# Gate values added element by element into a zeroed DRAM matrix, instead of one-hot products; last u tiles and v products in one program block

## The reference

```python
q = (xc @ w_q).reshape(ch, PEER_HEADS, 2, half)                 # 8 heads
s = jnp.einsum('thpd,hpnd->thpn', q, sub_keys)                  # 2 x 128 scores
v1, i1 = lax.top_k(s[:, :, 0], PEER_TOPK)                       # 16 of 128
v2, i2 = lax.top_k(s[:, :, 1], PEER_TOPK)
cand = (v1[..., :, None] + v2[..., None, :]).reshape(ch, PEER_HEADS, 256)
vals, ci = lax.top_k(cand, PEER_TOPK)
e = take(i1, ci // 16) * N_KEYS + take(i2, ci % 16)             # expert, 0..16383
g = jax.nn.softmax(vals, axis=-1)
act = jax.nn.gelu(jnp.einsum('td,thkd->thk', xc, u_tab[e])) * g
return jnp.einsum('thk,thkd->td', act, v_tab[e])
```

## Time and profile before

| What | us |
|---|---|
| median of 3 runs (3643.9 to 3649.4) | 3646.4 |
| the profiled execution's own time | 3651.8 |
| its span, first to last instruction | 3650.0 |
| PE busy | 3425.3 |
| DVE busy | 2373.7 |
| ACT busy | 1380.7 |
| POOL busy | 602.3 |
| layer 0, routing: first query product to its last u tile | 277.7 to 730.4 |
| layer 0, softmax and spread blocks | 734.3 to 1180.5 |
| layer 0, v products | 1201.5 to 1749.9 |
| layer 1, routing starts; last gelu of u | 2171.8 to 3072.0 |
| layer 1, projections (from the third on) start; attention starts | 1778; 1930.3 |
| layer 1, v products | 3092.4 to 3638.9 |

### The profile page before, as it was taken

The page is one execution under the profiler, slowest core; times in us unless marked ns, Lnnn a source line. Parts: engine busy times, 40 slices in busy tenths (PEclk is TensorE's granted clock), DMA queues, the critical chain, the costliest instruction groups (busy, mean ns, idle before and its releaser), DMA issues. The chain is left out here.

```text
span 3650.0 us, 51301 instructions
## 1 busy us (share of the span) xinstructions
PE 3425.3 (94%) x16516; PEld 2789.0 (76%) x16516; DVE 2373.7 (65%) x5172; ACT 1380.7 (38%) x2002; POOL 602.3 (17%) x545
## 2 busy tenths in 40 slices
PE   8779999989999799999899879999999997999998
PEld 6557888878888677778666568888788886778776
DVE  4545676755654688888536636767645554788887
ACT  3433333234444333333425623333234443333332
POOL 0000000000000755553000000000000002755551
PEclk9889999999999899999999989999999998999999
DMA  4113343334543999999311013434335444999997
GB/s 149 50 46 120 122 147 128 125 121 159 194 169 136 324 333 331 332 332 317 119 31 47 2 48 118 141 125 144 120 117 195 168 167 171 348 335 333 336 330 246
DMA packets 303862, 663.93 MB, mean 182 GB/s; under 512 B 34320, under 2 KB 159248, under 8 KB 302224
## 3 DMA queue, kind: packets, MB, share of 16 engines
q1 hardware_dynamic: 257264, 486.34, 38.6%
q0 software_dynamic: 45056, 134.38, 11.5%
q10 hardware_dynamic: 1440, 41.94, 2.8%
HBM read 551.40 MB, written 111.15 MB: 182 GB/s over the span
## 5 line engine op out<-in xcount | busy, mean ns | idle before, releaser
L398 PE MATMUL up_ps<-up_hhi,up_hi 128*128 128x512 f32 x2048 | 809.4, 395 | 7.9 <-PEq L1726 7.9
L398 PE MATMUL up_ps<-up_hlo,up_hi 128*128 128x512 f32 x2048 | 798.4, 390 | 0.0
L398 PE MATMUL up_ps<-up_hhi,up_lo 128*128 128x512 f32 x2048 | 798.2, 390 | 0.0
L1705 POOL DMA_INDIRECT ex_gz<-gelu,ga_atz x256 | 321.2, 1255 | 2572.6 <-POOLq L2106 2495.3
L389 DVE TENSOR_TENSOR up_lo<-up_raw,up_hi 128x1024 fp32r<-128x1024 f32 x256 | 313.5, 1225 | 585.5 <-ACT up_hi L385 574.5
L2268 PE MATMUL ex_psy<-ex_vh,ex_ah 128*128 128x512 f32 x1536 | 608.0, 396 | 67.4 <-DVE ex_al L2336 66.0
L2268 PE MATMUL ex_psy<-ex_vl,ex_ah 128*128 128x512 f32 x1536 | 599.7, 390 | 0.0
L2268 PE MATMUL ex_psy<-ex_vh,ex_al 128*128 128x512 f32 x1536 | 599.2, 390 | 0.0
L406 ACT ACTIVATE up_z<-up_ps 128x512 f32<-128x512 f32 x256 | 153.1, 598 | 897.4 <-PE up_ps L398 889.5
L398 PEld LDWEIGHTS up_ps<-up_hhi,up_hi 128*128 128x128 f32 x2048 | 385.9, 188 | 84.3 <-DVE up_lo L389 8.7
L398 PEld LDWEIGHTS up_ps<-up_hhi,up_lo 128*128 128x128 f32 x2048 | 385.0, 188 | 80.7
(11 more groups left out here) (355 smaller groups left out, 4162.6 us busy)
## 6 DMA issues: line engine op xcount, KB each, us to landing
up_raw<-in_uT SPq DMA_DIRECT2D x256, 512.0 KB, 3.3
ex_vr<-in_v SPq DMA_DIRECT2D x256, 512.0 KB, 5.6
gelu<-up_z SPq DMA_DIRECT2D x256, 256.0 KB, 2.0
ex_z<-gelu SPq DMA_DIRECT2D x256, 192.0 KB, 5.6
ex_gm<-gate_matrix SPq DMA_DIRECT2D x128, 320.0 KB, 6.7
gate_matrix<-sg_gbuf ACTq DMA_DIRECT2D x6, 4096.0 KB, 12.4
ro_wq<-in_peer_wq SPq DMA_DIRECT2D x32, 512.0 KB, 4.6
gate_matrix<-ga_last ACTq DMA_DIRECT2D x4, 4096.0 KB, 12.3
```

Source lines behind the costliest of these rows:

```text
L398: last = pe.matmul(self.ps[:, a, :], w[:, a, dc, :], h[:, dc, :], start=(dc == 0 and m == 0), stop=(dc == DC - 1 and m == 2))
L1705: pool.indirect_dma_start(z[:, j:j + 1], None, zmat.rearrange("p k (t a) -> (p k t) a", a=1), bass.IndirectOffsetOnAxis(ap=self.at_z[:, j: ...
```

## The change

1. **Zeroing.** In `front0` and `front1` POOL clears the small tile `ga_at`, and ACT issues eight writes (NZERO) of it, repeated, over the whole `gate_matrix`, one after each of the projections 2 to 9. The matrix now holds all 384 tokens in one layout (128 x 128 x 384), and SP waits for the writes at the end of the front block.
2. **Routing.** DVE computes the softmax and the addresses head by head (`shift`, `place`, `give`), with the exponential on ACT. POOL writes the gates of a head with 48 indirect DMAs (3 token tiles x 16), each of 128 single elements that are added to what DRAM holds (`scatter`). Before each head but the first, POOL waits until all additions of the heads before have landed. Six heads (ROUTED) are written within the routing block.
3. **Experts.** The blocks `gate_softmax` and `spread_gates` are gone. Their 64 u tiles stand at the head of the `experts` block, followed by the v products with no block end between. POOL writes the last two heads, gathers 8 v rows, waits for the gelus, then gathers as before. SP waits for all scatters before the first load of gates. The addition of a gathered row comes one iteration (four v tiles) later than before, and the six PSUM banks are added as each ends (`ended`).

```diff
+HW = TD * TOPK
+ROUTED = 6
+NZERO = 8
...
+    def zero_gates(self, act, gmat, n, signal):
+        z = self.zeros()
+        w = NK * SD // NZERO
+        rows = gmat.rearrange("p k t -> p (k t)")[:, n * w:(n + 1) * w].rearrange("p (r c) -> p r c", c=2 * HK)
+        act.dma_start(rows, bc(z.unsqueeze(1), [P, w // (2 * HK), 2 * HK])).then_inc(signal.sem, 16)
+
+    def scatter(self, pool, gmat, to, gates, h):
+        if h > 0:
+            pool.wait_ge(self.scattered.sem, self.scattered.base + 16 * HW * h)
+        for j in range(h * HW, (h + 1) * HW):
+            pool.indirect_dma_start(gmat.rearrange("p k (t a) -> (p k t) a", a=1),
+                                    bass.IndirectOffsetOnAxis(ap=to[:, j:j + 1], axis=0), gates[:, j:j + 1], None,
+                                    compute_op=ALU.add).then_inc(self.scattered.sem, 16)
...
 def route(...)
+            for h in range(ROUTED):
+                pool.wait_ge(given.sem, given.done(h))
+                ga.scatter(pool, gmat, to, gates, h)
...
+            def exps(h):
+                act.wait_ge(shifted.sem, h + shifted.done(0))
+                act.activation(share[:], share[:], ACT.Exp).then_inc(expd.sem, 1)
...
             def give(h):
-                at = bass.ds(h * TOPK, TOPK)
-                dve.tensor_copy(key1[:, :, at], keys[:, 0, :, :])
-                dve.tensor_copy(key2[:, :, at], keys[:, 1, :, :])
-                dve.tensor_copy(valsb[:, :, at], best[:]).then_inc(selected.sem, 1)
+                here = bass.ds(h * TOPK, TOPK)
+                place()
+                dve.scalar_tensor_tensor(out=spot[:, 0:TD, :], in0=at[:, 0:TD, :], scalar=float(SD), ...)
+                dve.tensor_scalar(spot[:, TD, :], at[:, TD, :], float(S), token[:, TD:TT], ALU.mult, ALU.add)
+                dve.tensor_copy(to[:, bass.ds(h * HW, HW)], spot[:, 0:TD, :].rearrange("p t k -> p (t k)"))
...
+                dve.wait_ge(expd.sem, h + expd.done(0))
+                dve.tensor_reduce(total[:], share[:], AX.X, ALU.add)
+                dve.reciprocal(total[:], total[:])
...
 def experts(...)
         def _(sp):
...
+            for a in range(GT):
+                load_v(a, a)
+            for t in range(2 * GT):
+                load_z(t, t // GT, t % GT)
+            sp.wait_ge(ga.scattered.sem, ga.scattered.base + 16 * PH * HW)
+            for par in range(2):
+                load_g(par, par)
...
         def _(pe):
+            with pe.Fori(0, (NK - G0) // GT) as i:
+                for a in range(GT):
+                    up.product(pe, i * GT + (G0 + a), a)
...
         def _(pool):
+            for h in range(ROUTED, PH):
+                ga.scatter(pool, gmat, to, gates, h)
+            for j in range(NV):
+                ga.gather_v(pool, gv, j)
+            for s in up.kept:
+                pool.wait_ge(s.sem, s.base + s.credit + 16 * NK // GT)
             for j in range(Z_AHEAD):
                 ga.gather_z(pool, gz, zmat, j)
+            for j in range(Z_AHEAD, HK):
+                ga.gather_z(pool, gz, zmat, j)
+                ga.gather_v(pool, gv, j)
...
         def _(dve):
-                        dve.tensor_tensor(blocks[:, 0:NTB - 1, :], blocks[:, 0:NTB - 1, :], gm[:, par, :, a, :], ALU.mult)
-                        dve.tensor_tensor(blocks[:, NTB - 1:NTB, :], blocks[:, NTB - 1:NTB, :], ga.last[...], ALU.mult)...
+                        dve.tensor_tensor(zz[:, par, a, :], zz[:, par, a, :], gm[:, par, a, :], ALU.mult).then_inc(s_["mul"].sem, 1)
```

More of the change, by code:

```diff
@@ L1743, in route @@
         keys = k.sb(c, f"ro_keys{l}", [P, 2, TT, TOPK])
+        share = k.sb(c, f"ro_share{l}", [P, TT, TOPK])
+        total = k.sb(c, f"ro_total{l}", [P, TT])
+        at = k.sb(c, f"ro_at{l}", [P, TT, TOPK])
+        spot = k.sb(c, f"ro_spot{l}", [P, TT, TOPK])
+        token = k.sb(c, f"ro_token{l}", [P, TT])
+        row = k.sb(c, f"ro_row{l}", [P, TOPK])
         psq = k.ps(c, f"ro_psq{l}", [P, 2, 512])
@@ L1977, in route @@
         s.passed(2 * PH)
-    selected.passed(PH)
+    for s in (selected, shifted, expd, given):
+        s.passed(PH)
 def reduced_angles(dve, ang, turns, out, quarter):
@@ L2269, in products @@
                                              start=(first and a == 0 and m == 0), stop=(final and a == GT - 1 and m == 2))
-                    last.then_inc(summed.sem, 1)
+                        if final and a == GT - 1:
+                            last.then_inc(s_["ended"].sem, 1)
+                    if not (final and a == GT - 1):
+                        last.then_inc(summed.sem, 1)
             products(0, 0, first=True)
@@ new lines, in _ @@
+            for j in range(ST):
+                up.gelu(act, G0 + j, j % GT)
+                up.high(act, G0 + GT + j, j % GT)
+                if j == ST - 1 and rope is not None:
+                    act.wait_ge(reduced.sem, reduced.done(1))
+                    act.activation(rope[:], rope[:], ACT.Sin)
+            with act.Fori(0, NP) as i:
+                for a in range(GT):
+                    up.gelu(act, i * GT + (G0 + ST + a), a)
+                    up.high(act, i * GT + (G0 + ST + GT + a), a)
@@ L2337, in iteration @@
                                           ALU.subtract).then_inc(weighted.sem, 1)
-            with dve.Fori(0, NI // 4) as i:
-                for half in range(4):
-                    iteration(i * 4 + half, half)
-            dve.wait_ge(summed.sem, summed.done(NK - 1))
+            for j in range(ST):
+                up.low(dve, G0 + GT + j, j % GT)
+                if j == 2 and rope is not None:
+                    dve.wait_ge(placed.sem, placed.base + 16)
+                    dve.tensor_copy(ang[:, 0, :], pos[:])
+                    dve.drain()
+                    dve.tensor_scalar(ang[:, 0, :], ang[:, 0, :], k.col("freq"), None, ALU.mult)
+                    dve.drain()
+                if j in (3, 5) and rope is not None:
+                    out = rope[:, (5 - j) // 2, :]
+                    reduced_angles(dve, ang[:, 0, :], ang[:, 1, :], out, (0.0, 0.25)[(j - 3) // 2]).then_inc(reduced.sem, 1)
+                    dve.drain()
+            with dve.Fori(0, NP) as i:
+                for a in range(GT):
+                    up.low(dve, i * GT + (G0 + ST + GT + a), a)
+            iteration(0)
+            with dve.Fori(0, NI // 4 - 1) as i:
+                for half in range(4):
+                    iteration(i * 4 + (half + 1), (i * 4 + half, half))
+            for half in range(3):
+                iteration(NI - 3 + half, (NI - 4 + half, half))
+            weigh(NI - 1, 3)
+            for q in range(4):
+                add_row(NI - 1, 3, q)
             for o in range(NO):
```

411 lines of the change are left out of this document (144 added, 267 removed).

## The result

| | before | after |
|---|---|---|
| median of the runs, us | 3646.3 (3643.9 to 3649.4, 4 runs) | 3797.1 (3792.0 to 3799.6, 4 runs) |
| ratio after / before | | 1.0415, 95% interval 1.0399 to 1.0431 |
| span of the profiled execution, us | 3650.0 | 3790.2 |
| PE busy, share of the span | 94% | 85% |

What follows compares the result with a forecast made beforehand. PE was taken to bound routing, DMA and PE within 5% the v products. From 3651.8 us, 240.5 went and 2, 4, 4 and 54 came: 3475.3, or 3470 as a median; range 3395 to 3575.

Steps and rivals of the forecast that it cites:

- the term that decides: Routing's block end waits for POOL to issue 288 scatters; delay 27 us a layer, 54 us in all.
- The laying out against DVE's rows: Routing: 288 scatters placed one by one, POOL's reads waiting for two-input DVE operations; they end at 763.
- Slower: Rival at routing's end: DMA engines doing eight additions each hold POOL; at 2.0 us a scatter 3831 us; chance 0.12.
- Dearer: Rival at routing's end: an addition needs more of POOL than a gather; pace 1.55, 3572 us; chance 0.14.
- turning point: Routing: the scatter pace, 1.68 us, at which the delay cancels the 115 us a layer won otherwise.
- One-hot products: Spread block: PE is the bound there, so all their time goes, 176.7 us in both layers.
- block ends: Between softmax and spread 11.3 us go, ahead of the v products 41.2 us.
- `give` and tokens: Routing: added DVE operations cost 4 us for `give` and 2 us for token numbers, both layers.
- No gap ahead of the v products: Experts block: SP issues the first tiles' loads two u tiles (10.9 us) ahead of need, so PE does not wait.
- Last additions: End of the v products: only the last one or two stay behind PE; 5 us won in both layers.
- Zeroing: Projections: zero writes slow weight loads beside them; 2 us a layer, 4 us, bounds 0 and 15 a layer.
- The v stage: v products: DVE's saving and 2% more gate bytes a tile costed at nothing, 10 us a layer either way.

Runs made afterwards that it cites:

- e5: Kernel after the change with scatters that write the gate plainly, without the addition: 3475.4 us.
- e6: Kernel after the change with each scatter on 64 partitions in place of 128, as many scatters: 3720.3 us.
- e3: Kernel after the change without any scatter and without the wait for them: 3403.7 us, ratio 0.9337.
- e4: Kernel after the change with each scatter replaced by a gather of one element a partition at the same addresses: 4120.1 us.
- e12: e4 plus a wait on POOL for the landing of all gathers before every fourth one: 3707.8 us.
- e7: Kernel after the change with four heads in routing and layer 1's zero writes issued by SP behind its last weight load: 3523.5 us.
- e9: e7 plus a landing signal for each 128 tokens, and layer 1's zero writes moved into attention behind the output weights' load: 3454.8 us.

## Why the prediction was wrong

**The step that failed** is the one called "the term that decides": a scatter was priced as a gather, 0.94 us and a pace of 1.24 to 1.46, because "the nearest rows are the gathers of one element a partition". They were the nearest rows, but they lacked the addition. Measured: 1.54 in place of 0.94, a mean pace of 1.91, a delay of 194 us a layer (first v product at 1279.9 with scatters and 1085.9 without) in place of 27. With the measured price the rest of the step holds: laid out again by the same rule with 1.54, the 288 scatters end at about 927 (an estimate from the same DVE rows), and they ended at 923.7. The upper bound was wrong in kind: I bounded the price by how far DVE's traffic can lengthen a gather, not by what the operation itself may need. The addition was named only for the rivals, at paces of 1.55 and 2.0, and the range ended at the first (3572, with 3575 as its upper end).

**The lesson of the same step that held.** The laying out against DVE's rows gave 763 for the last scatter of routing; with plain writes it is 765.3, and the time 3475 for a forecast of 3470. Contention adds 0.10 us on the mean, 1.054 against 0.952 for plain writes and 1.646 against 1.542 for adding ones in routing. A scatter of e5 beside a DVE operation with two SBUF inputs:

```profile
473.10 1.21 DVE L1961 TENSOR_TENSOR ro_wql<-ro_wq,ro_wqh 128x1024 fp32r<-128x1024 f32 x1
473.18 1.96 POOL L1700 DMA_INDIRECT gate_matrix<-pe_misc  x1 [0.30 <-issue]
```

It ends 0.83 us after the DVE operation does, and so do 51 of the 52 lengthened plain writes from 350 to 735; of the 40 lengthened adding ones 39 end 1.42 us after such an operation. My "0.94 + 0.14" was a misreading: the same lines of the earlier trace rows give 3094.48 + 1.74 - (3094.11 + 1.28) = 0.83. Laid out again with 0.83 the end is about 761, with 1.08 about 777, so the 763 belongs to the right number. The rule of the Trainium skill that I used for it ("SBUF — State Buffer", Who interferes with whom) says that such operations contend; these traces agree, with 0.10 us on the mean.

**The rivals.** *Slower* had the right place and nearly the right time, 3831 for 3797, with a wrong mechanism: it held POOL by the DMA engines, which are at 0.23 in the hole, and e6 excludes it. *Dearer* had the right mechanism ("an addition may need more of POOL than a gather") with too small a price. The estimate from the Trainium skill ("DMA: Bandwidth & Descriptors", Latency and other measured facts) of 1.6 us a scatter lies near 1.54, but by coincidence: it counted eight accesses in a row, and half of them cost 0.14 less, not 0.8. Its place in the text should have been a warning all the same, for it was the only figure for the accesses of an addition, and it stood just below the turning point.

**The other terms**, checked by e3, whose sum in my terms was 3416:
- One-hot products, transposes, block ends, `give` and tokens: forecast that the first v product comes at 736 + 348.2 = 1084.2; it comes at 1085.9. Right within 2 us a layer. The two heads left for the experts block were hidden.
- No gap ahead of the v products: right (0.23 us from the last u product to the first v product). Last additions: right (1.4 us behind PE).
- Zeroing at 2 us a layer: 0 and 20. I had bounded it at 15 and looked at the DMA share of 0.33. Eight writes 5.4 us apart drove that share to 1.05 and more, and the price was in the issuing queue that they held, which I had named ("ACT could fall behind") and not sized.
- The v stage at 0, ±10 a layer: 20 and 18 us won.
- Together: 38 won in the v stage, 16 lost by zeroing and 4 by the later first v products give 3416 - 18 = 3398, beside 3403.7 measured.

**The chances.** Faster 0.87 was far too sure. One unknown price decided the sign, the trace had no row of its operation, and its turning point of 1.68 lay only 0.25 above my value. With a price known no better than within a factor of two the slower case deserved 0.3 to 0.4.

## What to carry to other kernels

When one unmeasured price decides the sign, spread the chances over that price and not over the contention around it, and ask of the nearest row which part of the operation it lacks. Work on an engine off the critical path that must end within a block becomes the critical path at the block's end: balance such work between blocks by its measured pace, in pieces smaller than a head, until neither side waits there. A spare share of the DMA engines is an average: large writes issued faster than they can be moved fill them and hold the issuing queue for tens of microseconds. Issue them from a queue, and in a block, where nobody stands behind them, or further apart.

## What the runs showed of the hardware

- An indirect DMA of one element on each of 128 partitions keeps POOL for 0.95 us, reading or writing DRAM, and 1.54 us when it adds (e4, e5, after); with 64 partitions the adding one takes 1.40 (e6). The next starts 0.30 us later.
- Gathers of single elements issued every 1.25 us can nearly stop the other engines (e4, 470 to 490: a matmul every 2.80 us, DVE and ACT idle); plain writes at the same pace do not (PE is busy for all of 400 to 500 in e5), nor do gathers with a wait for all landings before every fourth (e12).
- A 3 MB write from a broadcast 1 KB source holds its issuing queue for 0.4 us when it comes 9 to 14 us after the one ahead (layer 0), and for 4 to 11 us when such writes follow every 5.4 us (layer 1), on ACT; on SP eight in a row held it for 61.5 and 70.5 us (e7, e9).
- POOL itself needed 0.1 us more on the mean for such an instruction beside routing's DVE work than beside an idle DVE. A lengthened one ended 0.83 us (plain, e5) or 1.42 us (adding, after) after a DVE operation with two inputs.
